# Two padding tiles of 64 bytes per partition around the split weights, and a third ahead of the attention tiles

## The reference

```python
h = LN(ALPHA*h + 0.5*swiglu(h))            # first block: 1024 -> 2816 -> 1024
h = LN(ALPHA*h + token_mixers(h))          # 1024 -> 3072, recurrent mixing, -> 1024
h = LN(ALPHA*h + cross_attention(h, mem))  # 256 memory tokens, 4 heads of 256
h = LN(ALPHA*h + 0.5*swiglu(h))
# second block: modulated RMS norm, h @ w_in (1024 -> 8704), neighbourhood
# attention over an 8 x 64 grid with 256 context tokens beside it, two
# convolution branches, three gated output products, and w_o
```

## Time and profile before

| | |
|---|---|
| median of three runs | 1708.47 us |
| span of the profiled execution | 1706.6 us |
| around the span (launch and end), by the difference | 1.9 us |
| TensorE matmuls | 8500, busy 1691.5 us |
| matmuls of `product`, L422 | 7146 |
| VectorE, ScalarE, GpSimd busy | 994.7, 683.6, 166.8 us |
| granted TensorE clock | 1.00 over the span (2.4 GHz) |

### The profile page before, as it was taken

One profiled execution on the slowest core, in us unless ns is written; L12 is line 12 of the kernel. 1 busy time (PEld: TensorE's weight loads), 2 busy tenths in 40 slices (PEclk: granted clock), 3 DMA queues, 4 the chain that ended last, 5 costly groups with the idle time before them and its releaser, 6 DMA issues.

```text
span 1706.6 us, 22901 instructions
## 1 busy us (share of the span) xinstructions
PE 1691.5 (99%) x8500; PEld 1394.7 (82%) x8500; DVE 994.7 (58%) x1341; ACT 683.6 (40%) x975; POOL 166.8 (10%) x158
## 2 busy tenths in 40 slices
PE   9999999999999999999999999999999999999999
PEld 7888888888787888888888888877778787788887
DVE  5333339987965784666333333457976869844442
ACT  4222232246454465434222223346454445732330
POOL 0000000112004521013000000013011020000000
DMA  5333247633122353223332233323333222243331
GB/s 216 98 98 98 91 138 231 222 121 119 52 98 66 109 182 137 67 82 123 98 98 94 92 130 117 109 87 118 85 99 95 86 83 86 74 123 109 104 109 62
DMA packets 51476, 188.05 MB, mean 110 GB/s; under 512 B 5776, under 2 KB 6288, under 8 KB 50512
## 3 DMA queue, kind: packets, MB, share of 16 engines
q1 hardware_dynamic: 44640, 161.50, 29.7%
q10 hardware_dynamic: 5184, 16.00, 2.9%
q0 software_dynamic: 1584, 9.60, 1.6%
HBM read 182.89 MB, written 4.19 MB: 110 GB/s over the span
## 4 chain that ended last, share of the span: by engine, by line
PE 89%; DVE 7%; ACT 2%; issue 1%; DMA 0%; POOL 0%; SPq 0%; DVEq 0%; ACTq 0%; POOLq 0%
PE proj L422 83%; DVE w_lo L414 1%; PE aux L1859 1%; PE aux L1846 1%; PE aux L1619 1%; PE aux L1836 1%; DVE y L2016 0%; ACT w_hi L407 0%; DVE score L1221 0%; DVE qk L1264 0%; DVE md L1242 0%; PE aux L566 0%; DVE qk L1265 0%; PE aux L1839 0%; DVE md L1241 0%
## 5 line engine op out<-in xcount | busy, mean ns | idle before, releaser
L414 DVE TENSOR_TENSOR w_lo<-raw,w_hi 128x1024 fp32r<-128x1024 f32 x300 | 380.5, 1270 | 388.8 <-ACT w_hi L407 382.0
L422 PE MATMUL proj<-a_hi,w_hi 128*128 128x512 f32 (+1 forms) x1536 | 600.8, 391 | 3.3 <-DVE a_lo L909 1.8
L422 PE MATMUL proj<-a_hi,w_lo 128*128 128x512 f32 (+1 forms) x1536 | 591.3, 385 | 0.0
L422 PE MATMUL proj<-a_lo,w_hi 128*128 128x512 f32 (+1 forms) x1536 | 591.0, 385 | 0.0
L407 ACT ACTIVATE w_hi<-raw 128x1024 fp32r<-128x1024 f32 x300 | 315.3, 1053 | 233.4 <-PE proj L422 164.3
L422 PEld LDWEIGHTS proj<-a_hi,w_hi 128*128 128x128 f32 x1536 | 288.5, 188 | 67.9 <-issue 5.8
L422 PEld LDWEIGHTS proj<-a_lo,w_hi 128*128 128x128 f32 x1536 | 288.7, 188 | 58.4 <-issue 2.9
L422 PEld LDWEIGHTS proj<-a_hi,w_lo 128*128 128x128 f32 x1536 | 288.5, 188 | 58.5
L422 PE MATMUL proj<-hid_hi,w_hi 128*128 128x512 f32 (+1 forms) x374 | 142.6, 381 | 0.0
L422 PE MATMUL proj<-hid_hi,w_lo 128*128 128x512 f32 (+1 forms) x374 | 140.9, 377 | 0.0
L422 PE MATMUL proj<-hid_lo,w_hi 128*128 128x512 f32 (+1 forms) x374 | 140.8, 377 | 0.0
(11 more groups left out here) (368 smaller groups left out, 2011.1 us busy)
## 6 DMA issues: line engine op xcount, KB each, us to landing
raw<-stream SPq DMA_DIRECT2D x303, 512.0 KB, 3.5
ctxk<-ada_in ACTq DMA_DIRECT2D x12, 512.0 KB, 3.7
ctxv<-ada_in ACTq DMA_DIRECT2D x12, 512.0 KB, 3.9
out<-h ACTq DMA_DIRECT2D x7, 256.0 KB, 2.0
h<-x_in SPq DMA_DIRECT2D x3, 512.0 KB, 8.7
btab<-rpb_in POOLq DMA_DIRECT2D x4, 384.0 KB, 3.5
cond_row<-cond_in ACTq DMA_DIRECT2D x1, 1024.0 KB, 5.9
side<-mem_in POOLq DMA_DIRECT2D x1, 1024.0 KB, 5.2
```

What stands on the lines that cost most here:

```text
L414: nc.vector.tensor_tensor(w_lo[:, st.slot], raw[:, st.slot], w_hi[:, st.slot].bitcast(F32), ALU.subtract).then_inc(lo_ready, 1)
L422: mm = nc.tensor.matmul(dst, a, b, start=start and n == 0, stop=stop and n == 2)
```

## The change

Two tiles that nothing reads or writes, `half_line` and `half_line_end`, stand before `w_hi` and behind `w_lo`, and a third, `half_line_x`, stands before `xp`. Each is 16 fp32, 64 bytes per partition. No instruction is added, removed or reordered.

```diff
         raw = sb("raw", [P, RING, SB * P])
+        sb("half_line", [P, 16])
         w_hi = sb("w_hi", [P, RING, SB * P], F32R)
         w_lo = sb("w_lo", [P, RING, SB * P], F32R)
+        sb("half_line_end", [P, 16])
         h = sb("h", [P, KD, T])
@@
             memv_hi, memv_lo = (sb(n, [P, MB, W5], F32R, ph) for n in ("memv_hi", "memv_lo"))
+            sb("half_line_x", [P, 16], F32, ph)
             xp = sb("xp", [P, 2, 2, M], F32, ph)
             xpt_hi, xpt_lo = (sb(n, [P, 2, MB, M], F32R, ph) for n in ("xpt_hi", "xpt_lo"))
             xs = sb("xs", [P, 3, 8, 2], F32, ph)
             ctx_hi = sb("ctx_hi", [P, KD, M], F32R, ph)
```

## The result

The kernel with the padding takes 1719.53 us (median of 4 runs, 1718.87 to 1721.57), the kernel before 1708.46 (4 runs, 1707.36 to 1708.8). The ratio is 1.0068 with a 95% interval of 1.0053 to 1.0082: slower by 0.7%. The prediction, 1663 us and faster, was wrong in sign and in size. The range of 1658 to 1711 missed by 8.5 us.

What follows compares the result with a forecast made beforehand. TensorE, busy 99% of the span, was taken as the bound. 47.0 us less 1.6 covered gave 45.4 us off 1706.6, 1661.2 us, and with 1.9 us for the runs' median 1663 us; range 1658 to 1711.

Steps and rivals of the forecast that it cites:

- The writes of the moved tiles: ScalarE and VectorE writing `w_hi` and `w_lo` at 64 past: between -10 and +4 ns in 500, counted as nothing.
- the transposes: 32 transposes of `xp` streaming `ident`, both now at 64 past: 0.2 us at most, taken as nothing.
- Weights at 64 past, moving activations at a multiple of 128: Main step, on `product`: every product gets the context's smaller fixed part, 6.67 ns less each, over 7050 matmuls.
- The 13.3 ns: Time of one `product` matmul beyond its columns, read as fixed and the same at 512 and 256 columns.
- the term of -47.0 us: Gain over all products but the context's 96: 7050 x 6.67 ns, before subtracting what waits would hide.
- different halves of the 128 bytes: Condition claimed for the context's 113.3 ns: next weights' load and moving operand lie in opposite 64-byte halves.
- the padding behind `w_lo`: Everything behind `w_lo` moves by 128 bytes and keeps its half: no effect.
- The covered part: 244 products in the mixing, memory attention and second block's attention head, in front of waits: 1.6 us gain nothing.
- No change: Rival: only the moving operand's own place counts; net -0.8 us, 1707.7 us, chance 0.30.
- Slower: Rival: strips stay at the unsettled 231.7 ns, 5.0 ns more per product; 1742 us, chance 0.15.
- More than forecast: Rival: the fixed part shrinks to the fp32 matmuls' 3.3 ns, 10.0 ns off each; 1640 us, chance 0.04.
- the first reading: For the context's 113.3 ns: load and moving operand in different halves of 128 bytes; gives every product 6.67 ns less.

Runs made afterwards that it cites:

- the mirror: Against the kernel before: split weights left at a multiple of 128 bytes, everything streaming past them moved to 64 past; 1719.8 us, ratio 1.0069.
- the table: No model, only sets of 72 split matmuls over pairs of places and narrower loads; 226.7 to 234.4 ns at 512 columns, 117.4 to 120.0 at 256.
- the history kernel: No model, six targets of 72 matmuls (difference 0, 64, 192; 256 and 512 columns), each behind seven predecessors; 113.33 or 117.78 ns at 256 columns, differences 64 and 192.
- the scan: No model, sets of 72 matmuls with the loaded operand at 0 to 496 bytes in steps of 16; lowest 226.7 ns at 512 columns, 113.3 at 256.
- the widths: No model, sets of 72 matmuls at differences 0, 64 and 192 and 16 widths from 160 to 512 columns; 111.7 ns at 192 columns, 226.7 to 233.4 at 512.
- the four kernels of sets: Four kernels without the model, only back-to-back sets of 72 `product` matmuls, no other engine at work: places, finer scan, predecessors, widths; paces measured instead of a kernel time.

## Why the prediction was wrong

**The bound was read rightly.** TensorE's list sets the end: its products became dearer by 12.7 us, and all but 1.7 us of it reached the span. The writes of the moved tiles (`w_lo` 1270 and then 1268 ns, `w_hi` 1053 both times) and the transposes cost nothing, as said.

**The step that failed** is in "Weights at 64 past, moving activations at a multiple of 128": "Since 13.3 ns was the same at both widths I take 6.67 at both." The 13.3 ns had been called a property of the matmul because two widths showed it. It is what difference 0 leaves beside the columns at widths like 512, 384, 320 and 256; at other widths from 240 up the same difference leaves 12.0 (272) to 16.7 (488), and difference 64 leaves 10.0 (272) and 20.0 (512). The 6.67 ns of the context is real at difference 64 and 256 columns, one of two paces there; at 512 columns the same difference costs 6.7. Carried to 7050 products it made the term of -47.0 us. Measured, the term is +12.3 us (+11.82 + 1.71 - 1.10 - 0.13), and +12.7 with the context's 0.40, which the forecast had at nothing.

**A second error stood beside it**: the forecast described the context by "different halves of the 128 bytes". The experiments show the difference in 256 bytes instead. The context had 64, the change made 192 of it, for the strips and the context both. So even at 256 columns the forecast's case wasn't made: "the context itself stays as it is" failed, 113.6 became 117.8. And `token_strip` was counted with the rest, though exchanging the roles turns 192 into 64, one of the dear places at 512 columns: 5.4 ns more in each of 316, where a gain of 6.67 had been forecast.

**Nor was the padding behind `w_lo` nothing**, as the forecast had it because everything behind it keeps its half. The two pads together set the difference: 64 bytes behind make it 192 and 1719.5 us, 192 bytes behind make it 64 and 1743.7.

**The covered part** was right in the mixing, with the other sign: from 418.4 to 474.3 us the products became 0.81 us dearer and the gaps 0.79 us shorter. The memory attention and the head of the second block's attention gave back 0.1 us together, and the rest fell at single waits elsewhere. That all gaps together make 1.67 us, where 1.6 had been expected, is luck.

**The rivals.** "No change" had the wide strips at 226.7 and the context at 120.0; it fell by 2.0 ns in 5972 matmuls, the size that the timeline's two decimals don't show in one step but show in sixty. Its own mechanism, the moving operand's place alone, is refuted by the mirror. "Slower" had the right sign, with a chance of 0.15, and said that it decides from 0.5 ns a product; measured were 2.0. Its price of 5.0 ns and 1742 us was too high for this change, and its mechanism is only half right: the new pace is settled, not the one behind a restart. With the other sign of the same shift it would have been close to the number, 1743.7. "More than forecast" has no support: nothing in 32 differences is below 226.66 ns at 512 columns.

**Ports, and the 2.5 ns.** The Trainium skill's page "SBUF — State Buffer", "Who interferes with whom", gives TensorE's moving operand and its loads independent ports. On other engines the runs agree with it: 226.7 ns with all other engines idle and with all at work. On its two own streams they don't show independence: with the loaded operand's address alone changed the pace goes from 226.7 to 234.4 ns. The warning that this rule gave, that the load's place can give no gain, was right in its result at 512 columns; at 256 columns the weights' shift alone gave 1.43 us. The Trainium skill's page "TensorE: Matmul & The Clock Gate", "Back-to-back issue gap", has 2.5 ns beside the columns; no pace of a split product with 512 columns came below 13.3, whatever the place.

**What the evidence before could have told.** It held one sample of a nonzero difference, at one width, and the forecast's gain rested on a width at which there was none. The unsettled 231.7 ns of the earlier trace rows was used for the first reading and as a rival's price, but not against the fixed part itself; it shows that the pace at 512 columns has more values than one with no address changed, which speaks against any fixed part that can be carried over.

**What stays open.** Why the pace repeats with 256 bytes, why multiples of 6.67 ns are preferred, why the dependence turns its sign with the width, and which of two paces a strip takes. Difference 192 at 512 columns had 229.0 in the changed kernel and 228.9 in the table and in the history kernel, but 233.3 twice in the scan and once among the widths; what decides that was not found. Whether the addresses act through the memory's layout or through the timing of the reads isn't shown. Each of the four kernels of sets ran once.

## What to carry to other kernels

A pace measured at one width and one pair of places is a sample and not a fixed part: before such a saving is multiplied by thousands of products, measure it at their own width, with their own operands, in a set of some seventy back to back. In this kernel, of the four differences tried in it (0, 64, 128 and 192), the split products of 512 columns are fastest when the loaded and the moving operand begin at the same place modulo 256 bytes, and padding ahead of either of them costs 0.7 to 2.1% of the whole; so whoever adds a small tile ahead of large ones should count bytes modulo 256. Compare paces over sixty steps, since two decimals of one step hide 2 ns.

## What the runs showed that was not expected

- With the same instructions, the same clock (1.00) and the same order, the kernel takes 1708.5, 1719.5, 1740.4 or 1743.7 us by where 64 to 256 bytes of padding lie.
- The pace of float32r matmuls with a load each depends on the loaded minus the moving address, in the scan with a period of 256 bytes: 226.7 ns at 0, 16 and 240, up to 234.4 at 96, with 512 columns; 120.0 at 0 and down to 113.3 at 64 and 192, with 256.
- At 256 columns and difference 64 or 192 two paces, 113.3 and 117.8 ns, last for a whole set, by what ran ahead of it.
- With padding that moves `side` alone, one execution's clock fell to 0.50 for 3.4 us behind a wait of 1.82 us, which cost an estimated 1.4 us, more than the 1.2 us that the padding could have given at best.
- A load of fewer columns isn't faster in sum at difference 0: 230.0, 229.9 and 231.7 ns with loads of 96, 64 and 32 columns, against 226.7 with 128. At difference 64, where 128 columns take 233.4 ns, they take 228.3, 232.6 and 231.0.
- A wider matmul can be the faster one: 508 columns take 227.5 ns, 512 take 226.7. At 192 and 160 columns the pace stops at 111.7 ns.
